# First head pair's combination on VectorE by token halves; transposed rows behind odd attention steps

## The reference

```python
for g, (win, d) in enumerate(DIL_PATTERNS):            # (128,1), (512,4), (2048,16)
    kk, vv = shared[g]
    o, l = dilated_group_attn(q[:, :, g], kk, vv, d, win // d)
    outs.append(o)
    lses.append(l)
o = jnp.stack(outs, axis=2)
alpha = jax.nn.softmax(jnp.stack(lses, axis=2), axis=2)
return (o * alpha[..., None].astype(o.dtype)).reshape(B, S, MAIN_W)
```

## Time and profile before

| what | value |
|---|---|
| median of 3 runs | 2090.73 us |
| lowest, highest | 2087.17, 2091.98 us |
| the profiled execution | 2087.22 us, span 2085.4 us, mean granted clock 0.985 |
| PE busy | 2007.2 us, 96% of the span |
| DVE busy | 1424.9 us, 68% |
| ACT busy | 931.0 us, 45% |
| POOL busy | 337.1 us, 16% |

### The profile page before, as it was taken

The page is one execution under the profiler, slowest core; times in us unless marked ns, Lnnn a source line. Parts: engine busy times, 40 slices in busy tenths (PEclk is TensorE's granted clock), DMA queues, the critical chain, the costliest instruction groups (busy, mean ns, idle before and its releaser), DMA issues.

```text
span 2085.4 us, 24972 instructions
## 1 busy us (share of the span) xinstructions
PE 2007.2 (96%) x9458; PEld 1604.6 (77%) x9458; DVE 1424.9 (68%) x1840; ACT 931.0 (45%) x1513; POOL 337.1 (16%) x188
## 2 busy tenths in 40 slices
PE   7997999999999999999999998999999999999997
PEld 6775787888888888887776665678788888888886
DVE  6567677576788875666454456477879988885665
ACT  6445343455546354342545556656522222234341
POOL 3643000111211000000000015020132333210001
PEclk9998999999999999999999998999999999999998
DMA  4228731365687876575121201123246654477544
GB/s 175 98 82 325 254 136 41 139 225 212 230 293 295 320 267 210 188 283 186 58 69 41 68 34 41 41 92 135 72 169 247 238 188 161 163 287 266 201 165 160
DMA packets 119895, 357.34 MB, mean 171 GB/s; under 512 B 10848, under 2 KB 12256, under 8 KB 114528
## 3 DMA queue, kind: packets, MB, share of 16 engines
q1 hardware_dynamic: 103312, 325.59, 43.7%
q10 hardware_dynamic: 16464, 30.15, 4.1%
HBM read 241.28 MB, written 114.43 MB: 171 GB/s over the span
## 4 chain that ended last, share of the span: by engine, by line
PE 74%; DVE 9%; DMA 8%; issue 4%; ACT 3%; SPq 1%; POOL 0%; ACTq 0%; POOLq 0%; DVEq 0%
PE PS L991 10%; PE PS L993 10%; PE PS L992 10%; PE PS L742 7%; PE PS L743 7%; PE PS L747 7%; PE PS L1009 5%; PE PS L1011 5%; PE PS L1010 5%; DMA s_keep<-ZS 2%; PE PTR L908 2%; PE PSC L878 2%; PE PX L895 2%; DMA TP<-x_mid 1%; DMA ZS<-in_wdn 1%
## 5 line engine op out<-in xcount | busy, mean ns | idle before, releaser
L1009 PE MATMUL PS<-RP,DH 128*128 128x512 f32 x616 | 241.2, 392 | 1.8 <-DVE RP L2264 1.8
L1010 PE MATMUL PS<-RP,DH 128*128 128x512 f32 x616 | 240.4, 390 | 0.0
L1011 PE MATMUL PS<-RP,DL 128*128 128x512 f32 x616 | 240.3, 390 | 0.0
L991 PE MATMUL PS<-BHT,SH 128*128 128x512 f32 x576 | 224.1, 389 | 0.0
L992 PE MATMUL PS<-BLT,SH 128*128 128x512 f32 x576 | 224.1, 389 | 0.0
L993 PE MATMUL PS<-BHT,SL 128*128 128x512 f32 x576 | 224.1, 389 | 0.0
L991 PE MATMUL PS<-BH,SH 128*128 128x512 f32 x432 | 168.2, 389 | 0.6 <-DVE SL L2165 0.6
L992 PE MATMUL PS<-BL,SH 128*128 128x512 f32 x432 | 168.1, 389 | 0.0
L993 PE MATMUL PS<-BH,SL 128*128 128x512 f32 x432 | 168.1, 389 | 0.0
L1009 PEld LDWEIGHTS PS<-RP,DH 128*128 128x128 f32 x616 | 116.0, 188 | 26.8 <-DVE RP L2264 3.1
L1136 ACT ACTIVATE DH<-DR 128x1408 fp32r<-128x1408 f32 x56 | 77.3, 1379 | 130.7 <-DMA DR<-s_keep 85.5
(11 more groups left out here) (332 smaller groups left out, 4654.0 us busy)
## 6 DMA issues: line engine op xcount, KB each, us to landing
SR<-in_wst SPq DMA_DIRECT2D x36, 1024.0 KB, 4.9
ZS<-in_wdn SPq DMA_DIRECT2D x32, 704.0 KB, 5.8
s_keep<-ZS SPq DMA_DIRECT2D x32, 704.0 KB, 4.7
DR<-s_keep SPq DMA_DIRECT2D x32, 704.0 KB, 5.3
inner<-TP SPq DMA_DIRECT2D x36, 512.0 KB, 4.3
WR<-in_w SPq DMA_DIRECT2D x35, 512.0 KB, 5.5
DR<-in_wdn SPq DMA_DIRECT2D x24, 704.0 KB, 4.7
RR<-t_keep SPq DMA_DIRECT2D x16, 1024.0 KB, 5.2
```

What stands on the lines that cost most here:

```text
L991: MM(BANK[bank], SH[b][:, w, c], BH[t][:, k, :], start=(k == 0), stop=False)
L1009: MM(bank, wh[:, i, :], rh, start=(i == 0), stop=False)
L1010: MM(bank, wh[:, i, :], rl, start=False, stop=False)
L1011: ins = MM(bank, wl[:, i, :], rh, start=False, stop=(i == KD - 1))
```

## The change

Two things change.

First, where transposed rows stand. `lse_rows` follow steps e + 3 and e + 5 of a slot's end in place of e + 3 and e + 6; `v_rows` follow steps q = 1 and 3 in place of 2 and 4; for the last stage (1, 1) and (3, 0) of the out jobs (m, q) in place of (1, 0) and (1, 2). A block is sent at the half-step just ahead of the next step (`k + 1 in places`), and no longer at the first one after its own. DVE's `log_sums` for r = 1 goes one step ahead too.

Second, the combination of the first pair. POOL's `combine` is gone; DVE has the differences, sums, weightings and scalings in `combine_first`, at the steps (n, q) of the table FIRST. Weighting, scaling, ACT's copy to CH and DVE's subtraction to CL are done by halves of 512 tokens, half 0 beside jobs 16 and 17, half 1 beside out jobs m = 1, 2, 3, 4. PE waits at the first out job for the same count 24 of `c_lo`, which now means half 0 of the three tiles, and for 27 at the first out job of token half 1. Counts of the semaphores after it move by 3.

```diff
         def rows_after(a):
-            return [(slot_ended(a, 3 + 3 * r), r) for r in range(2) if slot_ended(a, 3 + 3 * r)]
+            return [(slot_ended(a, 3 + 2 * r), r) for r in range(2) if slot_ended(a, 3 + 2 * r)]
...
                         if k in places:
                             step()
-                            if s and i == 0 and places.index(k) in (2, 4):
-                                rows_due.append((v_rows, s - 1, places.index(k) // 3))
-                        else:
+                            if s and i == 0 and places.index(k) in (1, 3):
+                                rows_due.append((v_rows, s - 1, places.index(k) // 2))
+                        elif k + 1 in places:
                             rows_now()
...
                     if m == 0 and h == 0:
                         pe.wait_ge(c_lo, 19 + 2 + 3)
+                    if m == 0 and h == 1:
+                        pe.wait_ge(c_lo, 19 + 2 + 6)
...
+                elif pair == 0:
+                    act.wait_ge(cmb_out, 3 * h + g + 1)
+                    A(CH[:, tiles[g], HALF[h]], OF[:, tiles[g], HALF[h]], ACT.Copy).then_inc(c_hi, 1)
...
-                    if n == 17 and q <= 2:
-                        combine(0, "split", q)
+                    if n == 17 and 1 <= q <= 3:
+                        combine(0, "split", q - 1, 0)
...
+            def combine_first(part, g, h=0):
+                t, c = 2 * g, HALF[h]
+                if part == "difference":
+                    dve.wait_ge(cmb_max, 2)
+                    V.tensor_tensor(QF[:, t, :], QF[:, t, :], MX[:, :], ALU.subtract).then_inc(cmb_diff, 1)
+                elif part == "sum":
+                    dve.wait_ge(cmb_diff, 3)
+                    dve.wait_ge(cmb_exp, g + 1)
+                    if g == 1:
+                        link(V.tensor_tensor(MX[:, :], QF[:, 0, :], QF[:, 2, :], ALU.add))
+                    else:
+                        V.tensor_tensor(MX[:, :], MX[:, :], QF[:, 4, :], ALU.add).then_inc(cmb_sum, 1)
+                elif part == "weighted":
+                    dve.wait_ge(o_free, 28)
+                    V.tensor_tensor(OF[:, t, c], OF[:, t, c], QF[:, t, c], ALU.mult).then_inc(cmb_part, 1)
+                elif part == "out":
+                    dve.wait_ge(cmb_inv, 2)
+                    dve.wait_ge(cmb_part, 3 * h + g + 1)
+                    V.tensor_tensor(OF[:, t, c], OF[:, t, c], MX[:, c], ALU.mult).then_inc(cmb_out, 1)
+                else:
+                    split_low(t, 22 + 3 * h + g, c)
+
+            FIRST = {(15, 0): (("difference", 0),), (15, 1): (("difference", 1),), (15, 2): (("difference", 2),),
+                     (15, 5): (("sum", 1),), (16, 0): (("sum", 2),),
+                     (16, 1): (("weighted", 0), ("weighted", 1)), (16, 2): (("weighted", 2),),
+                     (17, 0): (("out", 0), ("out", 1)), (17, 1): (("out", 2),),
+                     (17, 3): (("low", 0),), (17, 4): (("low", 1),), (17, 5): (("low", 2),)}
...
                     step()
-                    if (n, q) == (17, 3):
-                        for g_ in range(3):
-                            split_low(2 * g_, 21 + g_ + 1)
+                    for part, g_ in FIRST.get((n, q), ()):
+                        combine_first(part, g_)
...
+                        if h == 0 and q < 3 and m in (1, 2, 4):
+                            combine_first(("weighted", "out", "low")[(1, 2, 4).index(m)], q, 1)
...
-            def combine(part):
-                tiles = [2 * g for g in range(3)]
-                if part == 0:
-                    pool.wait_ge(cmb_max, 2)
-                    for t in tiles:
-                        G_.tensor_tensor(QF[:, t, :], QF[:, t, :], MX[:, :], ALU.subtract).then_inc(cmb_diff, 1)
...
-            for part in range(3):
-                combine(part)
             weights_to(NJ)
```

More of the change, by code:

```diff
@@ L1102, in _, with hook @@
                         pe.wait_ge(c_lo, 19 + 2 + 3)
-                    def hook(k, places=HOOKS[j], first=(h, m) == (0, 1)):
+                    if m == 0 and h == 1:
+                        pe.wait_ge(c_lo, 19 + 2 + 6)
+                    def hook(k, places=HOOKS[j], m=m + KT * h):
                         if k in places:
                             step()
-                            if first and places.index(k) in (0, 2):
-                                rows_due.append((v_rows, 5, places.index(k) // 2))
-                        else:
+                            if (m, places.index(k)) in VALUES:
+                                rows_due.append((v_rows, 5, VALUES.index((m, places.index(k)))))
+                        elif k + 1 in places or m == KT - 1 and k > places[-1]:
                             rows_now()
@@ L1676, in swap_quarter, with combine @@
                   scale=-SCALE if JOBS[j].name == "in" else 1.0).then_inc(swapped, 1)
-            def combine(pair, stage, g=None):
+            def combine(pair, stage, g=None, h=None):
                 tiles = [2 * g + pair for g in range(3)]
@@ L1715, in _ @@
                     step()
-                    if n and n % 3 == 0 and q in (2, 4):
-                        value_rows(n // 3 - 1, q // 3)
+                    if n and n % 3 == 0 and q in (1, 3):
+                        value_rows(n // 3 - 1, q // 2)
                     if n == 15 and 2 <= q <= 4:
@@ L1745, in _ @@
                         step()
-                        if (h, m) == (0, 1) and q in (0, 2):
-                            value_rows(5, q // 2)
+                        if (h, m) == (0, 3):
+                            combine(0, "split", q, 1)
+                        if h == 0 and (m, q) in VALUES:
+                            value_rows(5, VALUES.index((m, q)))
                     if (h, m) == (1, 0):
@@ L2600, in combine_last @@
                     for n, t in enumerate(tiles):
-                        dve.wait_ge(cmb_part, 3 + n + 1)
+                        dve.wait_ge(cmb_part, 6 + n + 1)
                         V.tensor_tensor(OF[:, t, :], OF[:, t, :], T[3], ALU.mult).then_inc(cmb_out, 1)
                 else:
-                    split_low(tiles[part - 5], 24 + part - 4)
+                    split_low(tiles[part - 5], 27 + part - 4)
             for n in range(19):
@@ L2644, in _ @@
                 for m in range(KT):
-                    for _ in HOOKS[J[("out", 1, m, (0, h))]]:
+                    for q in range(len(HOOKS[J[("out", 1, m, (0, h))]])):
                         step()
+                        if h == 0 and q < 3 and m in (1, 2, 4):
+                            combine_first(("weighted", "out", "low")[(1, 2, 4).index(m)], q, 1)
                     if (h, m) == (0, 7):
@@ L2732, in _ @@
                                  ALU.subtract).then_inc(v_lo, 1)
-            def combine(part):
-                tiles = [2 * g for g in range(3)]
-                if part == 0:
-                    pool.wait_ge(cmb_max, 2)
-                    for t in tiles:
-                        G_.tensor_tensor(QF[:, t, :], QF[:, t, :], MX[:, :], ALU.subtract).then_inc(cmb_diff, 1)
-                elif part == 1:
-                    pool.wait_ge(cmb_diff, 3)
-                    pool.wait_ge(cmb_exp, 3)
-                    link(G_.tensor_tensor(MX[:, :], QF[:, tiles[0], :], QF[:, tiles[1], :], ALU.add))
-                    G_.tensor_tensor(MX[:, :], MX[:, :], QF[:, tiles[2], :], ALU.add).then_inc(cmb_sum, 1)
-                    pool.wait_ge(o_free, 28)
-                    for t in tiles:
-                        G_.tensor_tensor(OF[:, t, :], OF[:, t, :], QF[:, t, :], ALU.mult).then_inc(cmb_part, 1)
-                else:
-                    pool.wait_ge(cmb_inv, 2)
-                    for n, t in enumerate(tiles):
-                        pool.wait_ge(cmb_part, n + 1)
-                        G_.tensor_tensor(OF[:, t, :], OF[:, t, :], MX[:, :], ALU.mult).then_inc(cmb_out, 1)
-            for part in range(3):
-                combine(part)
             weights_to(NJ)
```

15 lines of the change are left out of this document (8 added, 7 removed).

## The result

The first comparison gives 2070.42 us for the changed kernel (median of four, 2069.29 to 2075.44) against 2091.36 for the one before (2087.17 to 2092.1): ratio 0.9909, 95% interval 0.9888 to 0.993. The forecast was 2082, with 2076 as its lower end: right in sign, too small. Two later comparisons put the same program at 0.9938 and 0.993, so 13 to 15 us rather than 21.

What follows compares the result with a forecast made beforehand. TensorE works nearly all the time, so only stages holding it up can give anything back. Terms 3.5 + 2.0 + 1.6 + 2.0 + 1.0 - 1.8 + 0.5 gain 8.8 us: 2082 from the median 2090.73, range 2076 to 2091.

Steps and rivals of the forecast that it cites:

- Part 1: Transposed rows moved behind odd steps: TensorE's waits at their blocks shrink by 3.5, 2.0 and 1.6 us, plus 2.0 clock.
- the first blocks: First row block of each of four slots: waits shrink by the matmuls put ahead, 3.5 us gained, bounds 1.5 and 3.5.
- what stands behind blocks: TensorE's waits right behind row blocks, for ScalarE's VF and QF copies: 2.0 us gained, bounds 1.0 and 3.0.
- the second block: Second row block waiting 1.61 us while ScalarE awaits the cosine product: wait gone, 1.6 us gained, bounds 0 and 1.95.
- The clock term: Two stretches at 1.2 GHz behind waits of 2.79 and 1.61 us may not come: 2.0 us gained, bounds 0 and 3.5.
- The collision: GpSimd no longer slows VectorE's scalings before TensorE's 1.90 us wait at 1245.89: 1.0 us gained, bounds 0 and 1.9.
- The new wait: TensorE waits 5.8 us for the third low part at the first out job: 1.8 us lost, bounds 0 and 4.4.
- The rest of the out part: Smaller waits go and the second combination starts sooner, against added half-width operations: net +0.5 us, bounds -1.5 and +1.5.
- Rivals A and B: A: VectorE's fuller queue and late third low part, 2095, chance 0.10. B: waits only move, 2089, chance 0.23.

Runs made afterwards that it cites:

- rows_only: Kernel before with only the transposed rows moved, combination left on GpSimd: 2074.41 us against 2088.61, ratio 0.9932.
- v_only: Kernel before with only the values' transposed rows moved, log-sum rows and combination as before: 2082.18 us against 2087.26, ratio 0.9975.
- combine_only: Changed kernel with the transposed rows put back, so only the combination moves to VectorE: 2089.07 us against 2088.61, ratio 1.0001.
- cos_before: Kernel before with ScalarE's wait for the cosine product put behind a job's first step: 2088.71 us against 2087.26, ratio 1.0002.
- low_again: Second run of the changed kernel with half 0's low parts behind steps 1 to 3 of job 17: 2071.24 us against 2090.47, ratio 0.9911.
- after_third: The changed kernel itself, compared a third time with the kernel before: 2076.59 us, ratio 0.993.

## Why the prediction was wrong

**The waits of Part 1 came right in their sum, which was luck in part.** 3.5 for the first blocks, 2.0 for what stands behind blocks and 1.6 for the second block make 7.1 us. rows_only has 7.0 less idle (23.8 to 16.8). Within it the shares were off both ways. L853's 11.7 fell only to 8.4, not to about 6: slot 3 gives its gain back (1.70 and 0.68 there in rows_only), and a block at step 146 has 1.21. The probabilities' waits fell by 5.8 where I had 2.0, but the values' blocks now wait 2.1 us in place of 0.6. So part of the 8.1 us under VectorE's name in the earlier trace rows wasn't VectorE's alone, as v_only shows with 1.10 and 0.22 at VectorE's same slow scalings. ScalarE's row in before, beside the earlier trace rows:

```profile
1245.15 0.59 ACT L1702 ACTIVATE VF<-PTR 128x512 f32<-128x512 f32 x1
```

This copy of the values' block ends at 1245.74, the first of the two scalings from 1245.49 at about 1245.8, and TensorE goes on at 1245.89: the two waits end together, and the page names the later. No run took the block away altogether.

**The clock term was the step that failed.** It said that "the two stretches at 1.2 GHz behind them may not come", with "Bounds 0 and 3.5, I take 2.0." Measured in rows_only against before: 7.3 us (10.4 to 3.1 lost), outside my bound. I counted stretches only behind the waits that I had rows for. Those two, at 1122 and 1283, are gone and give 3.4. The stage has five, and the other three, at 1266, 1300 and 1317, lose 7.1 of the 10.4 and give 4.0. I priced 3.85 as keeping its stretch; it kept one, but 1.6 us in place of 2.5. The one behind 2.46 and 0.97 at 1300 I priced at nothing; rows_only loses 1.45 there, not 2.9. The one at 1317 is absent. The number was in front of me: a granted clock of 0.90 over 106 us is up to 10.6 us, and I asked for none of it where it went.

The 7.3 rests on one trace of each. For the whole change the three traces of after give 4.3 to 6.3. The medians allow an estimate that needs no trace's clock: rows_only is 14.2 us faster, of which 7.0 are idle time, 1.5 the last column of the ledger and 0.7 behind the stage, so about 5 are left for the clock (2 to 8 by its interval). The same for after, from 13.2 and 13.9 less 8.7, gives 4.5 and 5.2. So 2.0 was too small by about 3; that the term lies above my bound of 3.5 as well isn't certain.

By the Trainium skill (TensorE: Matmul & The Clock Gate, Part 1) the windows run free, and the term could be zero by it. That the outcome is not set by the length of the wait is shown here: behind slot 1's wait the first trace of after has the lower level, the third has not, at 1.86 and 1.89 us. The wait ends at 1119.66 in the first trace and at 1124.62 in the third, which has the full clock until 1263. The same window of 10 us in both:

```profile
1119.00:1129.00 10.00, 9.34 (x48) 6.71 (x50) 6.69 (x13) 4.85 (x12) 0.00 (x0) 0.83 0.30 96
```

```profile
1119.00:1129.00 10.00, 8.11 (x49) 5.96 (x50) 4.91 (x16) 8.47 (x19) 0.00 (x0) 1.00 0.00 1
```

That stretch, 1.7 us, is in 9 of 14 traces, before's among them, and absent in combine_only behind a wait of 2.81; so 1.7 of the 7.3 may be chance. More may be: combine_only, which keeps 2.81, 3.85 and 1.60 us of the old waits, loses 5.0 to the clock where before loses 10.4 and cos_before 11.2. The rule speaks for a wider term on both sides, not for zero.

**A term was missing.** Busy time at full clock, the last column, fell by 1.5 us in rows_only and by 2.3 in after, and I had nothing for it. TensorE's idle time in the stage comes in 31 pieces in before, 24 in rows_only and 19 in after. A wide matmul counts as busy for 0.39 to 0.40 us, while the next one starts after 0.23; ahead of a stop the other 0.16 are lost too, under the name of busy time. An estimate from these counts is 7 x 0.16 = 1.1 and 12 x 0.16 = 1.9 us, most of the term. No run tests it.

**The collision**, 1.0 with bounds 0 and 1.9: idle time of steps 122 to 130 falls by 1.65 in combine_only (1.90 is gone) but only by 0.2 between rows_only and after. The later blocks had already taken most of that wait (2.48 us idle there in before, 1.31 in rows_only); the two gains overlap, and I added them.

**The new wait**, -1.8 with bounds 0 and -4.4: the wait is 5.41 for 5.8. Against rows_only, steps 138 to 148 are 2.0 to 2.5 us longer, 1.5 of it idle. In low_again they are 3.7 to 4.2 shorter than in after, and 1.6 shorter than in rows_only. Right in mechanism and size. **The rest of the out part**, +0.5: steps 148 to 158 are 1.5 us longer than in before and 0.5 longer than in rows_only, and 0.66 come back behind them: small, and of the other sign. Rivals A and B fell: TensorE's idle time fell by 5.7, and VectorE's 14 us of added work, new wait included, cost 1.5 us between rows_only and after_third, two traces without the stretch in slot 1.

**The whole.** The stage by these terms: 7.0 + 7.3 + 1.5 for the rows, less 1.5 to 3.4 for the combination with its wait, makes 12.4 to 14.3, and 0.7 come behind it, against a forecast of 8.8; that is 2076 to 2078 from the median of before. Up to the scores of step 124 (1240 us in before) after is 3.4 to 5.0 us shorter in its traces, as forecast (3 to 6); behind them it is 9.0 to 9.6 shorter, where I had 3 to 6 and where four of the five stretches lie.

The other part of the miss, from there to 2070.42, is not the change. Programs that are the same up to step 64 reach it anywhere from 1063.54 us (after) to 1069.61 (cos_before), and take 748.3 to 752.9 us behind step 158. Of this the lower clock level takes 4.3 to 8.9 us ahead of the stage and 2.5 to 6.5 behind it, by the same sum; behind it that is most of the spread, ahead of it idle time (33.9 to 40.4) varies as much. Four executions of after gave 2070.42, twelve later ones medians of 2075.44 and 2076.59. Why the first four were low stays open.

## What to carry to other kernels

Before pricing a moved wait, list every stretch of the stage at the lower clock level and ask of each whether the wait ahead of it stays: here the clock was worth about 5 us by the medians, beside 7 for the waits, and forecast at 2. Where two producers share one bank, put the block that can wait just ahead of a step that begins with other work; the gap chosen was worth 10.2 us by the medians, and the place within the gap another 4.0 (7.6 and 8.2 in single traces, with their clock). A wait reported under another engine's name behind such a block can shrink with it. When work is moved onto the engine that feeds the next phase's first matmul, its last piece has to stand ahead of that engine's long chain (3.9 and 4.2 us of the stage here).

## What was not expected of the hardware

GpSimd also held a VectorE product with both inputs in SBUF. Two 512-wide products in after, the first with GpSimd idle, the second beside its split of the weights:

```profile
1249.80 1.28 DVE L2602 TENSOR_TENSOR OF<-OF,QF 128x512 f32<-128x512 f32 x2
...
1270.01 2.44 DVE L2606 TENSOR_TENSOR OF<-OF,MX 128x512 f32<-128x512 f32 x2
```

1.28 us for the one pair, 2.44 for the other. The Trainium skill (SBUF — State Buffer, Who interferes with whom) says that such an operation is locked out as well, and the trace agrees here. The earlier trace rows had seemed of two minds: the rotation's last addition took 1.93 us beside GpSimd's split. Three rows of before clear this up, the same addition with GpSimd idle, the split beside the addition, and one split alone:

```profile
1231.18 2.03 DVE L2562 TENSOR_TENSOR QF<-TP,TP 128x1024 f32<-128x1024 f32 x1
...
1295.86 4.04 POOL L2684 TENSOR_TENSOR WL<-WR,WH 128x512 fp32r<-128x512 f32 x2 [15.19 <-ACT WH L1136]
...
1308.55 1.28 POOL L2684 TENSOR_TENSOR WL<-WR,WH 128x512 fp32r<-128x512 f32 x1 [8.65 <-ACT WH L1136]
```

The addition takes about 2 us by itself. It had begun at 1295.54, ahead of the split, and it was GpSimd that lost, 4.04 us for two in place of twice 1.28. With eleven operations of GpSimd less the loss from such meetings was small all the same: TensorE has no wait between 1259.42 and 1286.25 in after.
